# Eight high-part products, then eight low-part products, in each weight unit of a split-precision matmul stream

## The reference, cut to what matters

```python
hn = rmsnorm(h, norm_mix_w[i])
z, xbc, dt_raw, u, g_a, g_b = jnp.split(hn @ w_in[i], splits, axis=-1)
y_a = mamba2_mixer(z, xbc, dt_raw, ...)        # ends in y @ w_proj
y_b = s5_mixer(u, ...)                         # ends in y @ w_glu
merged = jax.nn.sigmoid(g_a) * y_a + jax.nn.sigmoid(g_b) * y_b
h = h + merged @ w_out[i]
hn = rmsnorm(h, norm_ffn_w[i])
h = h + conv_glu_ffn(hn, w_up[i], conv_w, conv_b, w_down)
return rmsnorm(h, norm_final_w)
```

## Time and profile before

| | |
|---|---|
| median of 3 runs | 1716.89 us |
| span of the profiled execution, first to last instruction | 1715.5 us |
| TensorE (PE) busy | 1705.5 us, 99% |
| weight loads (PEld) busy | 1475.1 us, 86% |
| VectorE (DVE) busy | 1363.7 us, 79% |
| ScalarE (ACT) busy | 959.8 us, 56% |
| GpSimd (POOL) busy | 192.4 us, 11% |
| mean DMA rate | 190 GB/s |

### The profile page before, as it was taken

How to read it: one execution, slowest core, us unless ns; L and a number is a source line. 1 busy time by engine, 2 the same in 40 slices (tenths; PEclk the granted TensorE clock), 3 DMA queues, 4 the chain that set the end, 5 groups by cost and what they waited for, 6 DMA issues and landing times.

```text
span 1715.5 us, 30542 instructions
## 1 busy us (share of the span) xinstructions
PE 1705.5 (99%) x10110; PEld 1475.1 (86%) x10110; DVE 1363.7 (79%) x1901; ACT 959.8 (56%) x1247; POOL 192.4 (11%) x330
## 2 busy tenths in 40 slices
PE   9999999999999999999999999999999999999997
PEld 8888888888888888888888888888888888888886
DVE  7999999999999996556876688888888888544544
ACT  7766666666566665655655555444445444444432
POOL 7645312230000000000001000000000000000000
PEclk9999999999999999999999999999999999999999
DMA  7655555555556656555566565555565555655553
GB/s 251 218 181 174 188 187 176 176 166 188 169 204 227 204 195 196 185 195 184 189 229 191 186 192 187 183 184 185 193 195 191 183 181 189 197 189 192 187 191 114
DMA packets 96088, 325.76 MB, mean 190 GB/s; under 512 B 16784, under 2 KB 17216, under 8 KB 95904
## 3 DMA queue, kind: packets, MB, share of 16 engines
q1 hardware_dynamic: 88736, 311.12, 54.9%
q0 software_dynamic: 6576, 12.99, 2.5%
q10 hardware_dynamic: 720, 0.93, 0.2%
HBM read 321.77 MB, written 2.17 MB: 189 GB/s over the span
## 4 chain that ended last, share of the span: by engine, by line
PE 99%; DVE 0%; ACT 0%; issue 0%; DVEq 0%; POOL 0%; POOLq 0%
PE psum L1492 64%; PE psum L1494 31%; PE psum L1549 1%; PE psum L1581 1%; PE psum L1537 1%; PE psum L1504 0%; PE psum L1606 0%; PE psum L1582 0%; PE psum L1499 0%; DVE vn L1463 0%; PE psum L1637 0%; PE psum L1509 0%; PE psum L1597 0%; PE psum L1638 0%; PE psum L1598 0%; PE psum L1682 0%
## 5 line engine op out<-in xcount | busy, mean ns | idle before, releaser
L920 DVE TENSOR_TENSOR wlo<-raw,whi 128x1024 fp32r<-128x1024 f32 x580 | 710.0, 1230 | 294.7 <-ACT whi L525 293.0
L525 ACT ACTIVATE whi<-raw 128x1024 fp32r<-128x1024 f32 x580 | 611.2, 1058 | 435.6 <-PE psum L1494 418.2
L1492 PE MATMUL psum<-act,whi 128*128 128x512 f32 x1792 | 566.1, 397 | 0.0
L1492 PE MATMUL psum<-nw,whi 128*128 128x512 f32 x1536 | 483.2, 396 | 0.0
L1494 PEld LDWEIGHTS psum<-act,wlo 128*128 128x128 f32 x1792 | 336.6, 188 | 79.6
L1494 PE MATMUL psum<-act,wlo 128*128 128x256 f32 x1792 | 352.3, 278 | 0.0
L1494 PEld LDWEIGHTS psum<-nw,wlo 128*128 128x128 f32 x1536 | 288.5, 188 | 68.2
L1494 PE MATMUL psum<-nw,wlo 128*128 128x256 f32 x1536 | 301.8, 278 | 0.0
L1492 PEld LDWEIGHTS psum<-act,whi 128*128 128x128 f32 x1792 | 272.8, 189 | 7.7 <-issue 5.8
L1492 PEld LDWEIGHTS psum<-nw,whi 128*128 128x128 f32 x1536 | 233.9, 189 | 0.8 <-DVE wlo L920 0.4
L1492 PE MATMUL psum<-ff,whi 128*128 128x512 f32 x688 | 216.1, 395 | 0.0
(11 more groups left out here) (220 smaller groups left out, 1454.8 us busy)
## 6 DMA issues: line engine op xcount, KB each, us to landing
raw<-in_w_up SPq DMA_DIRECT2D x176, 512.0 KB, 4.3
raw<-in_w_zx SPq DMA_DIRECT2D x96, 512.0 KB, 3.3
raw<-in_w_down SPq DMA_DIRECT2D x88, 512.0 KB, 4.2
raw<-in_w_gate SPq DMA_DIRECT2D x64, 512.0 KB, 4.2
raw<-in_w_proj SPq DMA_DIRECT2D x48, 512.0 KB, 3.3
raw<-in_w_bc SPq DMA_DIRECT2D x32, 512.0 KB, 3.3
raw<-in_w_glu SPq DMA_DIRECT2D x32, 512.0 KB, 3.2
raw<-in_w_out SPq DMA_DIRECT2D x32, 512.0 KB, 4.1
```

Of the source, the lines that this page charges most:

```text
L525: fn(whi[:, s, :], raw[:, s, :], ACTF.Copy).then_inc(hi_ready, 1)
L920: V.tensor_tensor(wlo[:, s, :], raw[:, s, :], whi[:, s, :], ALU.subtract).then_inc(lo_ready, 1)
L1492: mm(psum[:, b + t, :], whi[:, s, cols(t)], x, start=first, stop=False)
```

## The change

In every unit but those of u0, the eight H products of the four row blocks are issued first, and then the eight L products, in the same order of k and t. The unit's waits stand where they stood, at its start. Only in u0 does the loop still go k by k (many = 1), with its waits. `late_tile` is as before.

```diff
                 s, b = n % RING, 2 * (g % 2)
-                for k in range(4):
+                tiles, many = range(2), 1 if name == "u0" else 4
+
+                def cols(k, t):
+                    return slice(k * L + t * P, k * L + t * P + P)
+
+                def moving(k):
                     row = 4 * q + k
+                    return act[:, row + (KT if name == "down" and row >= KT else 0), :]
+                for k0 in range(0, 4, many):
+                    ks = range(k0, k0 + many)
                     if name == "u0":
-                        pe.wait_ge(xwlo_ready, row + 1)
-                        pe.wait_ge(half_lo if k < 2 else lo_ready, n + 1)
-                    x = act[:, row + (KT if name == "down" and row >= KT else 0), :]
-                    first, last = q == 0 and k == 0, q == quads - 1 and k == 3
-                    tiles = range(2)
-
-                    def cols(t):
-                        return slice(k * L + t * P, k * L + t * P + P)
-                    for t in tiles:
-                        mm(psum[:, b + t, :], whi[:, s, cols(t)], x, start=first, stop=False)
-                    for t in tiles:
-                        ins = mm(psum[:, b + t, L:2 * L], wlo[:, s, cols(t)], x[:, 0:L], start=False, stop=last)
+                        pe.wait_ge(xwlo_ready, 4 * q + k0 + 1)
+                        pe.wait_ge(half_lo if k0 < 2 else lo_ready, n + 1)
+                    for k in ks:
+                        for t in tiles:
+                            mm(psum[:, b + t, :], whi[:, s, cols(k, t)], moving(k), start=q == 0 and k == 0, stop=False)
+                    for k in ks:
+                        for t in tiles:
+                            ins = mm(psum[:, b + t, L:2 * L], wlo[:, s, cols(k, t)], moving(k)[:, 0:L], start=False,
+                                     stop=q == quads - 1 and k == 3)
                 ins.then_inc(unit_used, 1)
```

## The result

The changed kernel takes 1720.41 us (median of 15 runs, 1720.2 to 1721.14) where the kernel before took 1716.95 us (15 runs, 1716.75 to 1717.89) beside it: a ratio of 1.002 with a 95% interval of 1.0012 to 1.0028. It is 3.5 us slower. That is small, but clear of the noise (the fastest of its runs is slower than the slowest of the kernel before), and it lies just outside the 1713.5 to 1720.3 us that the prediction called no change. The profiled execution took 1720.41 us, its span is 1718.8 us.

A forecast was written before the change was run, and what follows sets the result against it. The prediction took TensorE's own stream of products, busy 1705.5 of 1715.5 us, as the bound. Its four terms summed to 0 against the profiled span; with 1.4 us around it the forecast was 1716.9 us, range 1698 to 1735 us.

The forecast's parts named there:

- Term (1): Products, loads and columns in the changed units: none added or removed, 0 us.
- Term (2): Steps between products in a unit, reordered: 8 x 233 + 8 x 115 = 2784 ns before and after, 0 us.
- The bounds from the shortest and longest records: All products in changed units at their kind's shortest recorded length: 1689 us; all at the longest: 1754 us.
- The load rival: Runs of eight L outrun weight loads, 5.2 ns slip for six L a unit: 18 us slower, 1735 us; chance 0.24.
- The change-of-kind rival: Fewer H/L changes in a unit save 3.9 ns a pair: 18 us, 1699 us; most of the faster case's 0.36.
- Term (3): Waits at a unit's start and end stay; splits and weight DMA stay covered, with 6 us to spare.
- Term (4): Seams to the plain float32 pieces: units still begin with an H and end with an L, 0 us.
- The page's gaps: Long runs reaching N / 2.4 + 2.5 ns, 325 ns a pair against 348: -107 us, 1610 us; chance 0.02.

The follow-up runs named there:

- low_192: The changed kernel with 192 moving columns in place of 256 in every L product outside u0: 1684.13 us.
- low_96: The changed kernel with L products outside u0 loading 96 stationary columns in place of 128, but for the last row block of a group: 1705.57 us.
- one and one: The changed kernel reordered to alternate H, L outside u0, banks changing from pair to pair (1731.68 us) or one tile's bank after the other (1731.96 us).
- two and two: The order of the kernel before, two H then two L in each row block: 1716.95 us; with all of tile 0 first, then tile 1: 1717.09 us.
- high_384: The changed kernel with 384 moving columns in place of 512 in H products outside u0, but for the first of a group: 1595.93 us.
- high_96: The changed kernel with H products outside u0 loading 96 stationary columns in place of 128, but for a group's first and last row block: 1719.04 us.
- mix_a: The changed kernel reordered outside u0: row block 0 of each unit two H, two L, row blocks 1 to 3 alternating H, L: 1722.04 us.
- mix_d: The changed kernel reordered outside u0: each unit H, H, then L and H in turn, L last: 1734.51 us.

## Why the prediction was right or wrong

**The bound** was right: TensorE's own stream for 99%, and no wait of another engine above 0.5 us came or went.

**Term (1)**, nothing added or removed: right, 10110 instructions and the same lines.

**Term (2)** said that what a step costs "depends on the product that is running and hardly on the next", and so that the order is worth 0. The sum came within 3.5 us, but the reason is false: the cost of a product depends on several products before it. H went from 233 to 230 ns in the mean and L from 115 to 119. The step that failed is the extrapolation from a pair to a run of eight, in which every product keeps the mean price of its kind, 233 and 115. The rows of the kernel before could not show what a long run does, as they held only runs of two. They could have warned, though: by its records the gaps there are H 233, 236, 233, 231 and L 116, 113, 113, 119, so that a price already depended on the place, and the prediction's "about 120 ns for L to L" and "about 110 for L to H" are not what they say. The bounds from the shortest and longest records, 1689 and 1754 us, held, and the two directions were in them: in the changed kernel the median record of H is 393 ns, the shortest of before, and that of L is 283 ns, the longest of before.

**The load rival** is what happened to the L products, nearly in its numbers. It said that from the fourth load on L would slip by 5.2 ns, 18 us in all, and that L would then stand "about 120 ns apart from the third on". It is 120 ns from the third on, 30 ns a unit, 17.3 us. Its cause, loads that can't keep 115 ns for long, is not borne out: loads of 128 columns keep 112 ns, in low_192 and in the L1676 row of the kernel before. That a shorter load takes 17 ns off eight L (low_96) shows that the load has a part all the same. The transposes' loads that the prediction read as "about 100 ns apart" start 59 ns apart once and then 109 to 110 by the records; they too are faster than 115, so the reading did no harm.

**The change-of-kind rival** is what happened to the H products in size: 24 ns a unit, 13.9 us, where it said 18 us. Its cause was wrong. The 5.2 ns of late_tile are neither a price of a change of kind nor one of the bank: one and one can also run at 346.6 ns a pair, below two and two, and runs of four are dearer than both runs of two and of eight.

So the two rivals, each given alone, came together and nearly cancelled. That the time came within 3.5 us of the forecast is luck: it comes from this balance and not from the mechanism. By the prediction's own sign ("A median outside 1713.5 to 1720.3 refutes the zero in (2)") 1720.41 us refutes the zero, if barely; a third case, both at once, should have been among the rivals, since nothing made them exclude each other. Why an H gets cheaper and an L dearer deep in a run stays open.

**Term (3)**, the cover of the splits: right. Waits of H loads for wlo fell from 2.2 to 1.5 us. **Term (4)**, the seams: the units' medians alone explain the 3.5 us, so nothing is left for the seams.

**The page's gaps**, 325 ns for a pair: the nearest that any order came is 346.6 ns. The 2.5 ns over the columns in the Trainium skill ("TensorE: Matmul & The Clock Gate", section "Back-to-back issue gap") are 13.3 ns here, for fp32r products each with its own load. The 107 ns for a load of 128 columns that the Trainium skill's formula gives (same page, section "LDWEIGHTS (loading the stationary operand)") is 112 ns where the load binds (low_192, and L1676 in the kernel before).

## What to carry to other kernels

Where a stream of products already filled TensorE, as here, reordering them was worth from 0.1% less time to 1.0% more, and the costs of single steps from one product to the next did not add up: read the start-to-start distances by place in the sequence, look for where they settle, and forecast a new order from those places. This gave 1725.6 for a measured 1727.3, and 1715.5 for a measured 1715.2; it has its limit where an order has more than one rhythm, as one and one was forecast 8 us too high. Look also for a row that shows one resource alone, as L1676 shows the loads, before a rival is priced. A result near zero is to be split by kind of product before it is called no effect; here 14 us saved and 17 us lost lay behind 3.5. And a long run can pay for one size and save on another: here L went from 115 to 119 ns in the mean, H from 233 to 230.

## What the runs showed of the hardware

- **A settled fp32r product costs its columns at 2.4 GHz plus about 13.3 ns**: 173.3 (high_384), 227 and 120 ns (changed kernel) for 384, 512 and 256 columns, with loads of 128. Products with a load of 96 did not settle at one value (L in low_96, H in high_96). Sixteen products of a unit would be 8 x (226.7 + 120) = 2773 ns, and that is just what one and one takes in its short rhythm. The orders can be told apart by what they pay beyond that: runs of sixteen 10 ns a unit, pairs 14, eights 20, fours 34, one and one 0 or 46 to 57.
- **The same instructions have more than one stable rhythm.** One and one ran at 2773 or at 2830 ns a unit within one execution, and kept either for hundreds of microseconds. What picks it, and whether it can be forced, was not found; two tries failed (mix_a, mix_d). If it could be forced for the whole stream, 14 ns less a unit than two and two would be some 8 us, an estimate.
- **Weight loads run beneath products on the same 128 rows**: in the changed kernel a load's record starts 2 to 5 ns behind the start of a product and ends inside that product's record. The pace they can keep is about 112 ns for 128 columns (low_192, L1676), although each is recorded as 188 to 192 ns long.
- **Fewer stationary columns don't speed up a product that its moving columns bind** (high_96: 1719.04 us), but they do shift the pattern of the gaps around it.
